# Attention in one run of 160 steps of 128 queries, with the row sums applied to the output through a product with the identity

## The chip, the core and the metric

The kernel runs on one core of a Trainium2 chip. The metric is the device time of one execution in microseconds; given is the median of the runs. TensorE's granted clock has two levels, 2.4 GHz (written 1.00) and 1.2 GHz (0.50).

## What is computed

The reference is a two-layer backbone over 1024 latent tokens and 256 context tokens, all in float32. The change lies in the even layer's mixer, which has two kinds of attention side by side, eight heads each: grouped queries with 64 dimensions a head and two shared key heads, and a low-rank form with 96 dimensions (64 + 32) and a key for each head. Latent queries see all 1280 tokens, context queries only the 256 context tokens. Cut to what matters:

```python
def attend(q, k, v, scale):
    s = jnp.einsum('bhgqd,bhkd->bhgqk', q, k).astype(jnp.float32) * scale
    p = jax.nn.softmax(s, axis=-1).astype(v.dtype)
    return jnp.einsum('bhgqk,bhkd->bhgqd', p, v)
```

Around it stand input and output projections, norms and an MLP, and a second layer of long convolutions and a state-space scan. They make up most of the time and are not touched.

## The kernel before

`attention` (L1039) works heads in pairs: four pairs of the first kind, then four of the second. The loop `for kind in range(2)` (L1083) opens a stage of its own for each kind, with its own tiles and semaphores and a barrier at its end. Each pair has 20 steps. A step is one head with 128 queries against all their keys; four steps (two heads, two halves of 256 queries) make a block. Steps 0 to 15 of a pair are wide (1280 keys), steps 16 to 19, the context queries, narrow (256 keys). Here "step" counts within the pair where a number below 20 is given.

What a step does, in the order of its data:

- Scores (L1151, TensorE): products with the query block as weights, in parts of 512, 512 and 256 keys, into three of PSUM's banks 0 to 5 (two sets by the step's parity). To keep float32 precision, queries and keys are split into a high and a low part; the first kind takes two products a part (its low query part shares the rows of the high one), the second kind three.
- Row maximum (L1209, VectorE), negated, out of the score banks.
- Exponential (L1265, ScalarE), into one of three buffers `probs`, with the row's sum beside it.
- Reciprocal of the sum (L1215) and scaling of the probabilities (L1217), both VectorE.
- Turning (L1165, TensorE): ten transposes of 128 x 128 in groups of four, four and two, each group into one of two banks, 6 and 7; ScalarE copies each group out (L1240). A group waits until the last but one user of its bank has been copied out.
- After the four steps of a block, the mix (L1177, TensorE): for each of 10 key tiles and both heads a product with 64 columns of `v` as weights and 256 columns of turned probabilities, the two heads in the two halves of the partitions of one bank; ScalarE copies the result into `mixed` (L1247).

Each engine's order is a loop over x, written out by hand. TensorE in turn x: the scores of step x (behind exponential x-2), the mix if one is due, the turning of step x-2. VectorE: maximum x, then reciprocal and scaling of x-1. ScalarE: the mix's copy, the three turning copies of x-2, exponential x, which also waits until the transposes of x-3 have read its buffer (L1261).

The next pair's queries and keys come in items: three of the first kind, four of the second. SyncE loads an item (L1123) and, once a pair, the values (L1130, L1132); ScalarE rounds it to the high part (L1230), VectorE subtracts to get the low part (L1199). Items stand in the loops at steps 5, 8, 11 (and 14) of a pair (`split_at`, L1107): ScalarE rounds behind exponential i, VectorE splits behind reciprocal and scaling of i-1. The last pair of each kind has none. The items of a kind's first pair come before its first step.

Each product in float32 (not those of rounded parts) leaves two records in the trace, a transpose one. Of products that the comparison in the prediction touches, L1619 and L1620 stand in the scan of the second layer, with 64 columns of weights and 128 moving columns, eight heads into alternating halves of the partitions, and L1569 copies a bank of 512 columns with VectorE.

Of the kernel before, what the change touches and what calls it, by code (L numbers as in the profile page):

```python
# [1038 lines left out]
def attention(nc, g, sc, out):  # L1039

    PAIRS = 4
    QB = 256

    steps = [(b, h, t) for b in range(TOK // QB) for h in range(2) for t in range(2)]  # L1050
    S, B = len(steps), TOK // QB
    PER_BLOCK = S // B
    ALL = [(pair, i) for pair in range(PAIRS) for i in range(S)]
    N = len(ALL)

    def keys_of(b):
        return (0, KTILES) if b < LAT // QB else (LAT // P, KTILES)

    def block_of(x):
        return steps[ALL[x][1]][0]  # L1060

    def width(x):
        lo, hi = keys_of(block_of(x))
        return (hi - lo) * P

    def turns(x):
        lo, hi = keys_of(block_of(x))
        return [(i, min(i + 4, hi)) for i in range(lo, hi, 4)]

    use = {}
    for x in range(2, N + 3):
        if x > 2 and (x - 2) % PER_BLOCK == 0:
            use["mix", (x - 3) // PER_BLOCK] = len(use)
        if x - 2 < N:
            for j in range(len(turns(x - 2))):
                use["turn", x - 2, j] = len(use)
# [4 lines left out]
    for kind in range(2):  # L1083
        rows = slice(0, (P, B_DK)[kind])

        items = (((0, 0), (0, 1), (1, 0)), ((0, 0), (0, 1), (1, 0), (1, 1)))[kind]
        I = len(items)
        COPIES = (2, 1)[kind]
        names = "raw_in0 raw_in1 v_in0 v_in1 rounded split scores maxed exped inverse probs filled emptied"
        with stage(nc, names) as (mem, sems):  # L1090
            raw_in, v_in, (rounded, split, scores, maxed, exped, inverse, probs, filled, emptied) = sems[:2], sems[2:4], sems[4:]
            raw = tile(nc, mem, "qk_raw", [P, 2, TOK])
            heads = len(items) - 2
            q_hi, k_hi, k_lo = (tile_r(nc, mem, f"{x}", [P, 2, n, TOK]) for x, n in (("q_high", 2), ("k_high", heads), ("k_low", heads)))
            q_lo = q_hi if kind == 0 else tile_r(nc, mem, "q_low_part", [P, 2, 2, TOK])
            v = tile(nc, mem, "v_pair", [P, 2, KTILES, 2, B_V])
            p = tile(nc, mem, "probs", [P, 3, TOK])
            pt = tile(nc, mem, "probs_turned", [P, 2, 2, KTILES, QB])
            neg_max, total, inv = (tile(nc, mem, f"row_{x}", [P, 4]) for x in ("max", "sum", "inv"))

            def source(pair, item):
                which, h = item
                if kind == 0:
                    return sc.qk_a[1 + pair][64 * h:64 * h + 64, :] if which == 0 else sc.qk_a[0][64 * (pair // 2):64 * (pair // 2) + 64, :]
                return (sc.q_b, sc.k_b)[which][2 * pair + h]

            def split_at(x):  # L1107

                pair, i = ALL[x]
                n, off = divmod(i - 5, 3)  # L1110
                return (pair + 1, n) if off == 0 and 0 <= n < I and pair + 1 < PAIRS else None

            with nc.Block() as block:
                @block.sync
                def _(sp):
                    for pair in range(PAIRS):
                        for n in range(I):
                            m = pair * I + n
                            if m >= 2:
                                sp.wait_ge(split, m - 1)  # L1120
                            for c in range(COPIES):
                                at = rows if kind == 1 else slice(64 * c, 64 * c + 64)
                                sp.dma_start(raw[at, m % 2, :], source(pair, items[n])).then_inc(raw_in[m % 2], 16)  # L1123
                        if pair >= 2:

                            sp.wait_ge(filled, use["mix", (pair - 1) * B - 1] + 1)
                        s = pair % 2
                        if kind == 0:
                            for h in range(2):
                                sp.dma_start(v[:, s, :, h, :], sc.v_a[:, :, 64 * (pair // 2):64 * (pair // 2) + 64]).then_inc(v_in[s], 16)  # L1130
                        else:
                            sp.dma_start(v[:, s], sc.v_b[:, :, 128 * pair:128 * pair + 128].rearrange("p j (h n) -> p j h n", h=2)).then_inc(v_in[s], 16)  # L1132

                @block.tensor
                def _(pe):
                    def scores_of(x):
                        pair, i = ALL[x]
                        b, h, t = steps[i]
                        s, q0 = pair % 2, b * QB + t * P
                        qs = slice(q0, q0 + P)  # L1140
                        lo, hi = keys_of(b)
                        parts = [(a, min(BANK, hi * P - a)) for a in range(lo * P, hi * P, BANK)]
                        if i == 0:
                            pe.wait_ge(split, I * (pair + 1))
                        if x >= 2:
                            pe.wait_ge(exped, x - 1)
                        kh = 0 if kind == 0 else h
                        passes = [(q_hi, k_hi), (q_hi, k_lo)] + ([(q_lo, k_hi)] if kind else [])
                        for j, (a, n) in enumerate(parts):
                            for m, (left, right) in enumerate(passes):  # L1150
                                mm = pe.matmul(g.ps[:, 3 * (x % 2) + j, 0:n], left[rows, s, h, qs], right[rows, s, kh, a:a + n],  # L1151
                                               start=(m == 0), stop=(m == len(passes) - 1))
                            if j == len(parts) - 1:
                                mm.then_inc(scores, 1)

                    def turn(x):
                        first = keys_of(block_of(x))[0]
                        for j, (lo, hi) in enumerate(turns(x)):
                            if j == 0:
                                pe.wait_ge(probs, x + 1)  # L1160
                            r = use["turn", x, j]
                            if r >= 2:
                                pe.wait_ge(emptied, r - 1)
                            for kt in range(lo, hi):
                                mm = pe.transpose(g.ps[:, 6 + r % 2, (kt - lo) * P:(kt - lo + 1) * P], p[:, x % 3, (kt - first) * P:(kt - first + 1) * P], g.ident[:])  # L1165
                            mm.then_inc(filled, 1)
# [1331 lines left out]
```

## Time and profile before

| | |
|---|---|
| median of 3 runs | 4337.72 us (4336.04 to 4343.98) |
| the profiled execution, own time | 4339.12 us |
| its span | 4337.3 us |
| TensorE products, busy | 3786.3 us (87%) |
| VectorE, busy | 1762.5 us (41%) |
| ScalarE, busy | 1252.4 us (29%) |
| mean granted TensorE clock | 0.933 |

The span runs from the first to the last instruction; the execution's own time is measured around it. Busy time is the union of an engine's instructions, and a product's record is longer than the time from its start to the next one's, since products are pipelined: for TensorE the distance of starts tells the pace.

### The profile page before, as it was taken

Reading aid. Unit: us, or ns where it says so; the run is one execution under the profiler, and the core shown is the slowest. Engines: PE = TensorE matmul, PEld = TensorE weight load, DVE = VectorE, ACT = ScalarE, POOL = GpSimd, SP = SyncE. Lnnn points to the kernel's source line nnn. Section 1 sums busy time; section 2 is a strip of 40 time slices with the busy share of each in tenths; the row PEclk is TensorE's granted clock in tenths of the full one; section 3 lists DMA queues with packets and bytes.
Section 4 is the critical chain, followed back from the end, with each engine's and each line's share of the span. In section 5 each row is a group of like instructions: output and inputs, shape, how many; then the busy total and the mean of one; then the engine's idle time right before and its main releaser. Section 6 shows DMA issues by size and latency. Waiting matters only on the chain. (4 is left out here: it accounts for less than half of the span.)

```text
span 4337.3 us, 44967 instructions
## 1 busy us (share of the span) xinstructions
PE 3786.3 (87%) x17768; PEld 2748.8 (63%) x17768; DVE 1762.5 (41%) x2399; ACT 1252.4 (29%) x2132; POOL 114.0 (3%) x80
## 2 busy tenths in 40 slices
PE   6987788789877999999987997759899778999997
PEld 3662466566656888888856685513344547888885
DVE  2223566455335333333354334952133234333334
ACT  3322577566433111111132132201100132221122
POOL 0000000000010000000010002200000010000001
PEclk8998899899988999999998998859999889999998
DMA  7623310200121111111122110021300121111112
GB/s 299 248 73 109 80 37 1 58 25 16 35 97 45 39 39 39 38 34 39 39 102 78 64 35 2 1 84 49 136 25 25 53 83 58 45 48 49 48 48 92
DMA packets 98139, 272.34 MB, mean 63 GB/s; under 512 B 18157, under 2 KB 33005, under 8 KB 93972
## 3 DMA queue, kind: packets, MB, share of 16 engines
q1 hardware_dynamic: 98004, 270.51, 18.8%
q8 instruction: 88, 1.44, 0.1%
q14 instruction: 47, 0.39, 0.0%
HBM read 220.41 MB, written 50.07 MB: 62 GB/s over the span
## 5 line engine op out<-in xcount | busy, mean ns | idle before, releaser
L569 PE MATMUL psum<-h_high,w_high 128*128 128x512 f32 (+1 forms) x1280 | 473.5, 370 | 51.7 <-DVE w_low L648 51.7
L569 PE MATMUL psum<-h_low,w_high 128*128 128x512 f32 (+1 forms) x1280 | 473.0, 370 | 0.0
L569 PE MATMUL psum<-h_high,w_low 128*128 128x512 f32 (+1 forms) x1280 | 472.5, 369 | 0.0
L582 PE MATMUL psum<-hid_low,w_high 128*128 128x512 f32 (+1 forms) x1280 | 471.5, 368 | 0.0
L582 PE MATMUL psum<-hid_high,w_high 128*128 128x512 f32 (+1 forms) x1280 | 471.3, 368 | 0.0
L582 PE MATMUL psum<-hid_high,w_low 128*128 128x512 f32 (+1 forms) x1280 | 470.8, 368 | 0.0
L513 PE MATMUL psum<-h_high,w_high 128*128 128x512 f32 (+1 forms) x944 | 367.8, 390 | 36.8 <-DVE w_low L506 24.6
L645 DVE TENSOR_TENSOR out<-out,psum 128x512 f32<-128x512 f32 x320 | 202.9, 634 | 463.2 <-PE psum L582 463.2
L513 PE MATMUL psum<-h_high,w_low 128*128 128x512 f32 (+1 forms) x944 | 349.4, 370 | 0.0
L513 PE MATMUL psum<-h_low,w_high 128*128 128x512 f32 (+1 forms) x944 | 349.1, 370 | 0.0
L595 ACT ACTIVATE w_high<-w_raw 128x1024 fp32r<-128x1024 f32 x126 | 132.7, 1053 | 663.2 <-PE psum L582 662.8
L569 PEld LDWEIGHTS psum<-h_high,w_high 128*128 128x128 f32 x1280 | 242.5, 189 | 93.7 <-DVE w_low L648 29.0
L635 DVE TENSOR_TENSOR hid_high<-hid_relu 128x512 fp32r<-128x512 f32 x160 | 102.3, 639 | 479.6 <-ACT hid_relu L610 479.6
L1209 DVE TENSOR_REDUCE row_max<-psum 128x1 f32<-128x1280 f32 (+1 forms) x160 | 204.2, 1276 | 184.8 <-PE psum L1151 180.6
L1165 PE MATMUL psum<-identity,probs 128*128 128x128 f32 x1344 | 214.3, 288 | 64.7 <-ACT probs_turned L1240 34.6
L569 PEld LDWEIGHTS psum<-h_low,w_high 128*128 128x128 f32 x1280 | 242.6, 190 | 40.3
L569 PEld LDWEIGHTS psum<-h_high,w_low 128*128 128x128 f32 x1280 | 242.4, 189 | 40.7
L582 PEld LDWEIGHTS psum<-hid_high,w_high 128*128 128x128 f32 x1280 | 241.4, 189 | 40.8
L582 PEld LDWEIGHTS psum<-hid_low,w_high 128*128 128x128 f32 x1280 | 241.4, 189 | 40.1
L582 PEld LDWEIGHTS psum<-hid_high,w_low 128*128 128x128 f32 x1280 | 241.1, 188 | 40.4
L610 ACT ACTIVATE hid_relu<-psum 128x512 f32<-128x512 f32 x160 | 89.0, 556 | 561.7 <-PE psum L569 561.7
L513 PEld LDWEIGHTS psum<-h_high,w_high 128*128 128x128 f32 x944 | 179.0, 190 | 76.7 <-DVE w_low L506 23.7
(312 smaller groups left out, 5539.2 us busy)
## 6 DMA issues: line engine op xcount, KB each, us to landing
w_raw<-in_ff_w_dram SPq DMA_DIRECT2D x128, 512.0 KB
ada_ring<-in_ada_w_dram SPq DMA_DIRECT2D x24, 2048.0 KB, 8.9
scratch_x<-x SPq DMA_DIRECT2D x6, 2048.0 KB, 7.2
x<-scratch_x SPq DMA_DIRECT2D x6, 2048.0 KB
x<-in_x_dram SPq DMA_DIRECT2D x4, 2048.0 KB, 11.4
w_raw<-in_w_out_dram SPq DMA_DIRECT2D x16, 512.0 KB
scratch_spectra<-spectrum_out SPq DMA_DIRECT2D x32, 256.0 KB, 2.0
filter_ring<-scratch_spectra SPq DMA_DIRECT2D x16, 512.0 KB, 3.7
```

The source lines that it names most:

```text
L513: mm = pe.matmul(out, x[:, k, :], y[:, k, a:a + n], start=(k == 0 and i == 0), stop=(k == KT - 1 and i == 2))
L569: mm = pe.matmul(g.ps[:, u % BANKS, 0:n], x[:, k, :], y[:, k, a:a + n], start=(k == 0 and i == 0), stop=(k == KT - 1 and i == 2))
L582: mm = pe.matmul(g.ps[:, BANKS + u % BANKS, 0:n], x[:, k * 2 + half, :], y[:, k, a:a + n], start=(k == 0 and i == 0), stop=(k == HT - 1 an ...
L595: act.activation(w_hi[:, slot], raw[:, slot], ACT.Copy).then_inc(w_rounded, 1)
L610: act.activation(relu[:, u % 2, 0:n], g.ps[:, u % BANKS, 0:n], ACT.Relu).then_inc(up_free, 1)
L635: dve.tensor_tensor(hid_hi[:, j, a:a + n], relu[:, u % 2, 0:n], relu[:, u % 2, 0:n], ALU.mult).then_inc(rounded, 1)
L645: dve.tensor_tensor(out[:, m, a:a + n], out[:, m, a:a + n], g.ps[:, BANKS + u % BANKS, 0:n], ALU.add).then_inc(down_free, 1)
L1165: mm = pe.transpose(g.ps[:, 6 + r % 2, (kt - lo) * P:(kt - lo + 1) * P], p[:, x % 3, (kt - first) * P:(kt - first + 1) * P], g.ident[:])
L1209: dve.tensor_reduce(neg_max[:, x % 4:x % 4 + 1], flat, AX.X, ALU.max, negate=True).then_inc(maxed, 1)
```

## The change

The two stages become one. Tiles are allocated once, with room for the larger kind, and all eight pairs run as one chain of 160 steps; a table gives each item a number over all pairs, so that the last pair of the first kind now carries the four items of the first pair of the second. A block is 128 queries of both heads, two steps; a mix comes every second step, with 128 moving columns.

The scaling of the probabilities goes. Instead, behind a block's mix, TensorE multiplies the identity by the reciprocals spread over 64 weight columns, which puts each query's reciprocal into its column, in columns 128 to 255 of the same bank. ScalarE copies the mix to `mix_raw`, VectorE multiplies it by that and writes `mixed`.

TensorE turns step x-3 in turn x of its loop and places the groups of transposes between the parts of the scores; ScalarE's exponential is that of step x-1 in turn x; VectorE copies out the first group of each step. The items stay at steps 5, 8, 11, 14: ScalarE rounds behind exponential i (in turn i+1), VectorE splits in turn i. Four semaphores take the place of `emptied`, so that a group of transposes or a mix waits for the engine that copied its bank.

```diff
-    PAIRS = 4
-    QB = 256
...
-    steps = [(b, h, t) for b in range(TOK // QB) for h in range(2) for t in range(2)]
+    PAIRS, KINDS = 4, 2
+    LAG = 3
+    HEADS = 2
+    B = TOK // P
+    S = B * HEADS
+    ALL = [(pair, i) for pair in range(KINDS * PAIRS) for i in range(S)]
...
-    for kind in range(2):
...
-        with stage(nc, names) as (mem, sems):
+    with stage(nc, names) as (mem, sems):
...
+                def bank_free(r):
+                    if r < 2:
+                        return
+                    key = user[r - 2]
+                    if key[0] == "mix":
+                        pe.wait_ge(mixed_out, key[1] + 1)
+                    elif key[2] == 0:
+                        pe.wait_ge(first_out, key[1] + 1)
+                    else:
+                        pe.wait_ge(turned_out, act_turns[key[1], key[2]] + 1)
...
+                def mix(y):
+                    pair, b, _ = step(2 * y)
+                    lo, hi = keys_of(b)
+                    r = use["mix", y]
+                    bank_free(r)
+                    pe.wait_ge(first_out, 2 * y + 2)
+                    if act_turns_until(2 * y + 1):
+                        pe.wait_ge(turned_out, act_turns_until(2 * y + 1))
+                    pe.wait_ge(v_in[pair % 2], v_total(pair))
+                    for kt in range(lo, hi):
+                        for h in range(HEADS):
+                            mm = pe.matmul(g.ps[64 * h:64 * h + 64, 6 + r % 2, 0:P], v[:, pair % 2, kt, h, :], pt[:, y % 2, h, kt, :],
+                                           start=(kt == lo), stop=(kt == hi - 1))
+                    pe.wait_ge(inverse, 2 * y + 2)
+                    for h in range(HEADS):
+                        at = (2 * y + h) % 8
+                        mm = pe.matmul(g.ps[64 * h:64 * h + 64, 6 + r % 2, P:2 * P], inv[:, at:at + 1].to_broadcast([P, 64]), g.ident[:], start=True, stop=True)
...
-                    for x in range(N + 3):
-                        if x < N:
-                            scores_of(x)
-                        if x > 2 and (x - 2) % PER_BLOCK == 0:
-                            mix((x - 3) // PER_BLOCK)
-                        if 2 <= x < N + 2:
-                            turn(x - 2)
+                for x in range(N + LAG + 3):
+                    late = 2 if x < N and kind_of(step(x)[0]) else 3
+                    if x < N:
+                        scores_of(x, 0, 1)
+                    turn_due(x, 0)
+                    if x < N:
+                        scores_of(x, 1, late)
+                    turn_due(x, 1)
+                    if x < N:
+                        scores_of(x, late, 3)
+                    if block_due(x) is not None:
+                        mix(block_due(x))
+                    turn_due(x, 2)
...
+                for x in range(N + LAG + 3):
+                    if 0 <= x - LAG < N:
+                        dst, src = turned_to(x - LAG, 0)
+                        dve.wait_ge(filled, use["turn", x - LAG, 0] + 1)
+                        dve.tensor_copy(dst, src).then_inc(first_out, 1)
+                    if x < N:
+                        dve.wait_ge(scores, x + 1)
+                        if x >= 4:
+                            dve.wait_ge(exped, x - 3)
+                        dve.tensor_reduce(neg_max[:, x % 4:x % 4 + 1], scores_flat(x), AX.X, ALU.max, negate=True).then_inc(maxed, 1)
+                    if block_due(x) is not None:
+                        y = block_due(x)
+                        pair, b, _ = step(2 * y)
+                        r = use["mix", y]
+                        dve.wait_ge(mix_copied, y + 1)
+                        dve.tensor_tensor(out[:, pair, b * P:(b + 1) * P], mix_raw[:, y % 2, :], g.ps[:, 6 + r % 2, P:2 * P], ALU.mult).then_inc(mixed_out, 1)
+                    if 1 <= x <= N:
+                        y = x - 1
+                        dve.wait_ge(exped, y + 1)
+                        if y >= 8:
+                            dve.wait_ge(filled, use["mix", (y - 8) // 2] + 1)
+                        dve.reciprocal(inv[:, y % 8:y % 8 + 1], total[:, y % 4:y % 4 + 1]).then_inc(inverse, 1)
+                    if x < N and split_at(x):
+                        split_item(*split_at(x))
...
-                            dve.tensor_scalar(p[:, y % 3, 0:width(y)], p[:, y % 3, 0:width(y)], inv[:, y % 4:y % 4 + 1], None, ALU.mult).then_inc(probs, 1)
...
+                for x in range(N + LAG + 3):
+                    if 1 <= x <= N:
+                        y = x - 1
+                        act.wait_ge(maxed, y + 1)
+                        if y >= 3:
+
+                            act.wait_ge(filled, last_turn(y - 3) + 1)
+                        if y >= 4:
+                            act.wait_ge(inverse, y - 3)
+                        act.activation(p[:, y % 3, 0:width(y)], scores_flat(y), ACT.Exp, bias=neg_max[:, y % 4:y % 4 + 1],
+                                       accum_out=total[:, y % 4:y % 4 + 1]).then_inc(exped, 1)
+                        if split_at(y):
+                            round_item(*split_at(y))
+                    for j in (1, 2):
+                        if j == 2 and block_due(x) is not None:
+                            y = block_due(x)
+                            r = use["mix", y]
+                            act.wait_ge(filled, r + 1)
+                            if y >= 2:
+                                act.wait_ge(mixed_out, y - 1)
+                            act.activation(mix_raw[:, y % 2, :], g.ps[:, 6 + r % 2, 0:P], ACT.Copy).then_inc(mix_copied, 1)
+                        if 0 <= x - LAG < N and j < len(turns(x - LAG)):
+                            dst, src = turned_to(x - LAG, j)
+                            act.wait_ge(filled, use["turn", x - LAG, j] + 1)
+                            act.activation(dst, src, ACT.Copy).then_inc(turned_out, 1)
```

## Rows read from the trace of the kernel before

**Rows 1.** Table of stretches: each engine's busy us (instructions), granted clock, DMA share, GB/s
```profile
456.00:1122.00 666.00, 554.61 (x3728) 416.21 (x3728) 381.95 (x508) 429.84 (x804) 0.00 (x0) 0.95 0.14 32
```

**Rows 2.** Timeline, wide steps of first kind: start, us, engine, line, count [idle before]
```profile
707.95 1.32 ACT L1265 ACTIVATE probs<-psum,row_max 128x1280 f32<-128x1280 f32 x1
...
711.45 4.54 PE L1177 MATMUL psum<-probs_turned,v_pair 128*64 128x256 f32 x40
715.92 1.78 PE L1165 MATMUL psum<-identity,probs 128*128 128x128 f32 x10
717.46 0.48 PE L1151 MATMUL psum<-k_high,q_high 128*128 128x512 f32 x1
...
718.71 1.03 PE L1165 MATMUL psum<-identity,probs 128*128 128x128 f32 x8
...
723.55 1.32 ACT L1265 ACTIVATE probs<-psum,row_max 128x1280 f32<-128x1280 f32 x1
```

**Rows 3.** Timeline, ScalarE, a block of the second kind
```profile
1055.66 1.32 ACT L1265 ACTIVATE probs<-psum,row_max 128x1280 f32<-128x1280 f32 x1
...
1073.50 1.32 ACT L1265 ACTIVATE probs<-psum,row_max 128x1280 f32<-128x1280 f32 x1
```

**Rows 4.** Timeline, the seam between the kinds
```profile
762.73 0.49 ACT L1265 ACTIVATE probs<-psum,row_max 128x256 f32<-128x256 f32 x1
...
785.04 0.79 PE L1151 MATMUL psum<-k_high,q_high 96*128 96x512 f32 x1 [19.09 <-DVE k_low L1199]
...
790.17 1.33 ACT L1265 ACTIVATE probs<-psum,row_max 128x1280 f32<-128x1280 f32 x1 [6.71 <-DVE row_max L1209]
```

**Rows 5.** Timeline, ScalarE: first and last exponentials of four pairs
```profile
623.02 1.33 ACT L1265 ACTIVATE probs<-psum,row_max 128x1280 f32<-128x1280 f32 x1 [0.92 <-DVE row_max L1209]
...
693.53 0.49 ACT L1265 ACTIVATE probs<-psum,row_max 128x256 f32<-128x256 f32 x1
...
696.48 1.33 ACT L1265 ACTIVATE probs<-psum,row_max 128x1280 f32<-128x1280 f32 x1 [0.93 <-DVE row_max L1209]
...
957.86 1.33 ACT L1265 ACTIVATE probs<-psum,row_max 128x1280 f32<-128x1280 f32 x1 [0.92 <-DVE row_max L1209]
...
1038.97 0.49 ACT L1265 ACTIVATE probs<-psum,row_max 128x256 f32<-128x256 f32 x1
...
1042.50 1.33 ACT L1265 ACTIVATE probs<-psum,row_max 128x1280 f32<-128x1280 f32 x1 [0.92 <-DVE row_max L1209]
...
1116.72 0.49 ACT L1265 ACTIVATE probs<-psum,row_max 128x256 f32<-128x256 f32 x1
```

**Rows 6.** Timeline, TensorE, scan of the second layer: first and last of eight rows
```profile
2706.28 0.45 PE L1619 MATMUL psum<-segments,x_dt 128*64 128x128 f32 x4 [0.36 <-DVE segments L1712]
...
2707.86 0.44 PE L1620 MATMUL psum<-exp_acs,states 128*64 128x128 f32 x4
```

**Rows 7.** Groups by line, VectorE, 2690 to 2760 us: busy us, mean ns, idle before
```profile
L1569 DVE COPY ssd_out<-psum 128x512 f32<-128x512 f32 x8 | 5.5, 684 | 0.0
```

**Rows 8.** Timeline, an item step of the first kind: rounding and split
```profile
504.45 1.27 ACT L1230 ACTIVATE q_high<-qk_raw 128x1280 fp32r<-128x1280 f32 x1
...
505.75 1.49 DVE L1199 TENSOR_TENSOR q_high<-qk_raw,q_high 64x1280 fp32r<-64x1280 f32 x1 [2.03 <-ACT q_high L1230]
```

**Rows 9.** Timeline, TensorE behind two of its longer stops, one in each kind
```profile
523.63 0.55 PE L1165 MATMUL psum<-identity,probs 128*128 128x128 f32 x3 [1.83 <-DVE probs L1217]
...
858.70 1.63 PE L1165 MATMUL psum<-identity,probs 128*128 128x128 f32 x8 [2.63 <-DVE probs L1217]
```

**Rows 10.** Table of stretches around such stops; the clock is the third number from the end
```profile
859.00:862.40 3.40, 3.40 (x19) 3.17 (x18) 1.88 (x5) 2.09 (x8) 0.00 (x0) 0.52 0.03 11
...
941.00:947.80 6.80, 5.25 (x24) 4.78 (x25) 3.69 (x9) 4.35 (x9) 0.00 (x0) 0.50 0.24 75
...
1026.30:1033.00 6.70, 6.00 (x28) 5.31 (x30) 2.87 (x7) 4.79 (x11) 0.00 (x0) 0.50 0.01 2
518.00:526.00 8.00, 4.60 (x30) 3.61 (x29) 6.21 (x7) 6.07 (x12) 0.00 (x0) 1.00 0.31 82
```

More of the change, by code:

```diff
@@ L1039, in attention @@
 def attention(nc, g, sc, out):
[L1047 to L1054 removed]
+    PAIRS, KINDS = 4, 2
[4 more added lines that the diff above has]
+    ALL = [(pair, i) for pair in range(KINDS * PAIRS) for i in range(S)]
+    N = len(ALL)
+    ITEMS = (((0, 0), (0, 1), (1, 0)), ((0, 0), (0, 1), (1, 0), (1, 1)))
@@ L1056, in keys_of, with kind_of, step @@
+    COPIES = (2, 1)
+    ROWS = (slice(0, P), slice(0, B_DK))
+    jobs = [(pair, n) for pair in range(KINDS * PAIRS) for n in range(len(ITEMS[pair // PAIRS]))]
+    job_of = {job: m for m, job in enumerate(jobs)}
+    def kind_of(pair):
+        return pair // PAIRS
+    def step(x):
+        pair, i = ALL[x]
+        return pair, i // HEADS, i % HEADS
     def keys_of(b):
-        return (0, KTILES) if b < LAT // QB else (LAT // P, KTILES)
-    def block_of(x):
-        return steps[ALL[x][1]][0]
+        return (0, KTILES) if b < LAT // P else (LAT // P, KTILES)
@@ L1062, in width, with raw_total @@
     def width(x):
-        lo, hi = keys_of(block_of(x))
+        lo, hi = keys_of(step(x)[1])
         return (hi - lo) * P
     def turns(x):
-        lo, hi = keys_of(block_of(x))
+        lo, hi = keys_of(step(x)[1])
         return [(i, min(i + 4, hi)) for i in range(lo, hi, 4)]
-    use = {}
-    for x in range(2, N + 3):
-        if x > 2 and (x - 2) % PER_BLOCK == 0:
[L1075 to L1078, printed above, removed]
+    def raw_total(m):
+        return 16 * sum(COPIES[kind_of(jobs[i][0])] for i in range(m % 2, m + 1, 2))
@@ new lines, in v_total, with block_due @@
+    def v_total(pair):
+        return 16 * sum(COPIES[kind_of(i)] for i in range(pair % 2, pair + 1, 2))
+    def block_due(x):
+        y, odd = divmod(x - LAG - 2, 2)
+        return y if not odd and 0 <= y < N // 2 else None
+    use, act_turns = {}, {}
+    for x in range(N + LAG + 3):
+        for j in range(3):
+            if j == 2 and block_due(x) is not None:
+                use["mix", block_due(x)] = len(use)
+            if 0 <= x - LAG < N and j < len(turns(x - LAG)):
+                use["turn", x - LAG, j] = len(use)
+                if j:
+                    act_turns[x - LAG, j] = len(act_turns)
@@ L1080, in last_turn @@
+    user = {r: key for key, r in use.items()}
     def last_turn(x):
         return use["turn", x, len(turns(x)) - 1]
-    for kind in range(2):
[L1084 to L1089, printed above, removed]
-        with stage(nc, names) as (mem, sems):
[L1091 to L1144, printed above, removed]
@@ L1145, in scores_of @@
                         if x >= 2:
                             pe.wait_ge(exped, x - 1)
[L1147 to L1166, printed above, removed]
@@ new lines, in scores_of @@
+                    kh = 0 if kind == 0 else h
+                    passes = [(q_hi, k_hi), (q_hi, k_lo)] + ([(q_lo, k_hi)] if kind else [])
+                    for j, (a, n) in list(enumerate(parts))[first:last]:
+                        for m, (left, right) in enumerate(passes):
+                            mm = pe.matmul(g.ps[:, 3 * (x % 2) + j, 0:n], left[at, s, h, qs], right[at, s, kh, a:a + n],
+                                           start=(m == 0), stop=(m == len(passes) - 1))
+                        if j == len(parts) - 1:
+                            mm.then_inc(scores, 1)
@@ new lines, in turn_due @@
+                def turn_due(x, j):
+                    if 0 <= x - LAG < N and j < len(turns(x - LAG)):
+                        turn(x - LAG, j)
+                for x in range(N + LAG + 3):
[11 more added lines that the diff above has]
+                    turn_due(x, 2)
```

188 lines of the change are left out of this document (107 added, 81 removed).

## The prediction

> **What bounds the kernel now.** The change touches attention alone. A table of stretches [rows 1] gives its part of the span, 456 to 1122 us: of 666 us matrix products are busy for 555, VectorE for 382, ScalarE for 430. No engine is full, so I looked for the wait that ends last in three places, each by the starts of the exponentials, one a step. **A steady block**: four steps of the first kind with one mix take 723.55 - 707.95 = 15.60 us [rows 2], of the second 1073.50 - 1055.66 = 17.84 [rows 3]. In the three steps without the mix the timeline shows TensorE stopping before its third group of transposes until a bank is copied out, and ScalarE with three copies and an exponential back to back; during the mix ScalarE has nothing to copy. TensorE sets one step and ScalarE's copies the other three. **The seam between the kinds**: the last exponential of the first kind starts at 762.73, the first of the second at 790.17, and TensorE is idle for 19.09 us of it [rows 4]. **The item steps**: three or four times in a pair a piece of the next pair's queries or keys is rounded by ScalarE and split by VectorE, and both queues stand behind it. From the first exponential of a pair to its last it is 70.51 us with three items and 66.25 without in the first kind, 81.11 with four and 74.22 without in the second [rows 4, 5].
>
> **The sum, part by part.** The profiled execution took 4339.1 us, 1.4 above the median of 4337.7. The sum is a difference, worked out within the profiled one and put on the median.
>
> *Mixing in blocks of 128 queries.* The 672 mix products become 1344 of half the width; each leaves two records. Today 40 records of 256 columns take 715.92 - 711.45 = 4.47 us, 0.112 each [rows 2]. The nearest row of the new shape, 64 weight columns against 128, is in the scan stage: two lines with 32 records of it together, from 2706.28 to 0.22 behind 2707.86, so 1.80 us, 0.056 each [rows 6]. 40 of them take 2.25 us, and column work stays the same: nothing gained or lost. The Trainium skill (TensorE: Matmul & The Clock Gate, Back-to-back issue gap) speaks against the change here: it says that a stream of weight loads and products of 128 columns keeps about 81 ns apiece. By that, as an estimate, the 2688 records would cost 67 us more; rows 6 disagree. *The product with the identity* adds four such records a block: 0.22 us in each of 80 blocks, all on TensorE. The reciprocals it reads were made long before, so I cost its wait at nothing.
>
> *Two steady steps.* First kind: scores 718.71 - 717.46 = 1.25 us, ten transposes 1.09 together (eight run for 1.03, the last one's own length among it, so I take 0.109 from start to start), so 4.68 for two steps; with 2.25 and 0.22 it is 7.15 us. With two turning banks some waits stay: a copy takes 0.6 to 0.7 us, and the group after next finds its bank full for 0.1 to 0.5. I laid the new queue orders out with these durations and find some 0.5 in two steps, 7.65 against 7.80 now. Second kind: nine products for six, scores 1.25 x 1.5 = 1.87, so 8.4 and 0.1 of waits, 8.5 against 8.92. There are 32 such pairs of steps of each kind: -5 and -13 us. Bounds: no wait left -38; 0.5 us more of waits in each two steps +14. I take -18, the layout being nearer the rows than either end, and +3.5 for the 16 narrow blocks, whose identity products buy nothing. VectorE loses a scaling of 1280 columns and gains a copy out of PSUM, 0.68 us [rows 7], and every second step a product of a quarter of its width, at most as much; ScalarE loses one copy of three. The maximum has the width of a split, 1.49 [rows 8], so VectorE has under 2.7 us of work in 3.8: cost nothing. TensorE covers it; with that cover gone VectorE would set 2.7 a step.
>
> *One run of 160 steps.* The 27.44 us at the seam become what lies between two pairs, 696.48 - 693.53 = 2.95 [rows 4, 5]: -24.5. Bounds: -24.5 and 0, if pair 3 cannot take its neighbour's pieces in time. I take -24.5, since other pairs do it. SyncE issues the same transfers in the same order, and none is moved past another.
>
> *Items.* Now 9 at (70.51 - 66.25) / 3 = 1.42 us and 12 at 6.89 / 4 = 1.72: 33 us. Afterwards there are 25, as pair 3 also carries the four of pair 4. This is where the new order hurts. VectorE meets the split of step i right behind that step's maximum and stands until ScalarE has rounded. ScalarE rounds behind exponential i, and that, through its wait for the buffer of three steps ago, cannot start before TensorE's last transposes of the same turn of the loop, nor, by its queue, before their copy. From there on: copy of 256 columns 0.3 (a fifth of the 1.32 of 1280), exponential 1.32, rounding until VectorE starts 505.75 - 504.45 = 1.30, split 1.49, and then the next step's first copy, 0.68, which was ScalarE's and now stands behind the split: 5.0 us with the ends overlapping by 0.1 [rows 2, 7, 8]. On TensorE the mix or the third transposes wait for that bank, and all else is queued behind. Before them TensorE has a step's scores and two groups, 2.1 us (2.5 to 2.7 in the second kind). So it stands 2.9 or 2.5 us, and 3.5 where the next step has a mix (items at steps 8 and 14), since ScalarE's own copies are then 0.6 behind. The first kind has 8 and 5 of these, the second 6 and 6: 8 x 2.9 + 5 x 3.5 + 6 x 2.5 + 6 x 3.5 = 77 us, net +44. Bounds: as dear as today, 25 x 1.5 = 38, net +5; nothing beside the chain, 25 x 5.0, net +92. I take the chain less the work beside it.
>
> Together: -18 + 3.5 - 24.5 + 44 = +5 us.
>
> *The clock.* In the narrow steps of the second kind TensorE stood for 2.63 us before 858.70, and the granted clock was half (0.5, 1.2 GHz) from 859.1 for 3.4 us; at the same place of the next two pairs it was half for 6.8 and 6.7. After a stop of 1.83 us before 523.63 it stayed 1.00 [rows 9, 10]. Of the new stops 13 of the first kind and 6 of the second are longer than 2.63, six a little shorter. I take 17 falls. In 3.4 to 6.8 us at half clock TensorE loses 1.7 to 3.4 where it is the limit; some of it runs in the next wait, so 2.1 each: +36 us. Bounds: no fall, 0; 25 falls at 2.8, +70.
>
> Forecast: +41 on 4337.7, **4379 us**.
>
> **Rivals.** (1) *The clock holds*: the new stops lie in dense work, the narrow steps in thin. For it: 1.83 us did nothing. Against it: all three such places in the second kind were answered. Then +5, 4343 us; chance 0.20. (2) *Faster: the item steps hide their chain.* Its place is VectorE's first copy, its price what that copy is late for its bank. At today's 1.5 us an item with the clock unmoved the sum is -18 + 3.5 - 24.5 + 5 = -34, 4304 us; it decides as soon as an item costs under 2.8 us. For it: today's items hide half of their work. Against it: today only the next maximum stands behind the split, then a bank does. Chance 0.10. (3) *Narrow products don't stream.* If a record keeps the 0.112 us of today's, the 2688 add 0.056 x 2688 = 150; half of that gives 4454 us. Against it: rows 6, with the same alternation of halves. Chance 0.05. The skill's 81 ns would be in this case. (4) *The seam stays*, since pair 4's pieces come late: 24 us more, 4403 us. Against it: their steps are 5, 8, 11 and 14 of 20. Chance 0.05.
>
> **Numbers.** The forecast keeps 0.60. A measurement of this kernel tells a change of 0.2% (8.7 us, 4329 to 4346) from none. Case 1 lies in that band for 0.14 of its 0.20, with 0.02 faster and 0.04 slower. Faster: 0.10 + 0.02 = 0.12; same 0.14; slower 0.60 + 0.04 + 0.10 = 0.74. The range goes down to 4338, which takes in most of case 1 and leaves out case 2, and up to 4402, the forecast with 59 of the clock's 70 us, which leaves out cases 3 and 4.
>
> **What would show it.** Mix records of 128 columns 0.056 us apart; TensorE idle for 2.5 to 3.5 us once behind each item and for over 1 us hardly elsewhere; VectorE's split waiting longer for the rounding than now; half clock behind most items; first-kind pairs some 80 us long, the last pair without items under 76. It is wrong if pairs with three items last under 75 us, if the clock stays full behind the items, or if mix records lie over 0.07 us apart.

## The result, and the profile after

| | before | after |
|---|---|---|
| median | 4336.88 us, 4 runs | 4383.66 us (4379.17 to 4388.61), 4 runs |
| ratio | 1 | 1.0103 [1.0087, 1.0119] |
| profiled execution, span | 4337.3 us | 4379.5 us (own time 4381.26) |
| attention, first score to last `mixed` | 648.2 us | 691.1 us |
| the rest of the kernel behind it | 3216.1 us | 3215.5 us |
| first exponential of a pair to the next pair's, first kind | 73 | 82 us |
| half clock behind a stop in attention | 3, in the narrow steps of the second kind | 23, behind 25 item stops |

The kernel became slower by 1.03%; 4379 had been forecast. All of it is in attention, +42.9 us. (The untouched rest lay between 3208 and 3220 us over the profiles of this study, so the experiments are read by attention's own length wherever the total is too coarse.)

Two words are used throughout. A *stop* is a stretch in which TensorE stands still and waits. A *fall* is a stretch at half clock that follows: the granted clock goes from 1.00 to 0.50 and comes back after 3.4 us, sometimes 6.8.

The page after, engines:

```profile
span 4379.5 us, 48447 instructions
PE 3825.9 (87%) x19432; PEld 2836.1 (65%) x19432; DVE 1752.0 (40%) x2479; ACT 1184.2 (27%) x2012; POOL 114.0 (3%) x80
```

Attention as a stretch, to be held against [rows 1]; then the stretch behind one item's stop, and behind the two stops, of 3.33 and 2.43 us, that no fall followed. Columns: length, busy us of TensorE, its weight loads, VectorE, ScalarE and GpSimd, granted clock, DMA share, GB/s.

```profile
456.00:1164.00 708.00, 593.81 (x5392) 503.10 (x5392) 371.44 (x588) 361.61 (x684) 0.00 (x0) 0.92 0.13 31
594.00:597.80 3.80, 3.39 (x36) 3.39 (x38) 1.75 (x2) 0.00 (x0) 0.00 (x0) 0.55 0.67 172
790.20:793.60 3.40, 3.23 (x48) 2.87 (x49) 1.71 (x3) 0.64 (x3) 0.00 (x0) 1.00 0.53 149
830.40:834.00 3.60, 3.59 (x29) 3.10 (x31) 2.60 (x4) 2.35 (x4) 0.00 (x0) 1.00 0.44 137
```

VectorE has 10 us less work than before and ScalarE 68 less, and the stretch is 42 longer. TensorE's busy time grew with it (554.6 to 593.8 us) and is 83 to 84% of it in both. No engine is fuller: something waits more. TensorE's waits say for what (in total, times, longest):

```profile
PE psum L1192 <- DVE probs_turned L1262: 43.5, 30, 3.0
PE psum L1206 <- DVE probs_turned L1262: 40.6, 19, 3.5
...
PE psum L1192 <- ACT probs_turned L1321: 0.8, 3, 0.3
```

84 us of idle TensorE end with the same instruction, VectorE's copy of a step's first group of transposes; 76 of them are the 25 stops behind items. ScalarE's copies, which set three of four steps before, end next to none. The timeline of one item (rows left out are marked; all engines, start and length; the idle time before and who ended it in brackets):

```profile
573.62 0.44 PE L1192 MATMUL psum<-identity,probs 128*128 128x128 f32 x2
574.09 0.38 ACT L1321 ACTIVATE probs_turned<-psum 128x256 f32<-128x256 f32 x1
574.37 1.33 ACT L1306 ACTIVATE probs<-psum,row_max 128x1280 f32<-128x1280 f32 x1
...
575.64 0.60 PE L1192 MATMUL psum<-identity,probs 128*128 128x128 f32 x4
575.68 1.27 ACT L1293 ACTIVATE q_high<-qk_raw 128x1280 fp32r<-128x1280 f32 x1
576.98 1.49 DVE L1254 TENSOR_TENSOR q_high<-qk_raw,q_high 64x1280 fp32r<-64x1280 f32 x1 [2.57 <-ACT q_high L1293]
578.50 0.69 DVE L1262 COPY probs_turned<-psum 128x512 f32<-128x512 f32 x1
579.25 0.44 PE L1192 MATMUL psum<-identity,probs 128*128 128x128 f32 x2 [3.00 <-DVE probs_turned L1262]
```

Read it downwards as one chain: TensorE's last transposes of a turn, their copy, the exponential, the rounding, the split, the copy that had to wait behind the split, and TensorE again. VectorE stood for 2.57 us with the bank's copy in its queue (its group of transposes had left TensorE at 575.64 + 0.60) and nothing to do but wait for ScalarE. From the start of the last transposes to the third transposes of the next turn it is 5.6 us, of which TensorE stands for 3.00.

A steady two steps of the first kind, by ScalarE's exponentials, and the seam between the kinds (before: [rows 2] and [rows 4]):

```profile
517.16 1.32 ACT L1306 ACTIVATE probs<-psum,row_max 128x1280 f32<-128x1280 f32 x1
520.15 1.33 ACT L1306 ACTIVATE probs<-psum,row_max 128x1280 f32<-128x1280 f32 x1 [0.21 <-DVE row_max L1267]
524.81 1.33 ACT L1306 ACTIVATE probs<-psum,row_max 128x1280 f32<-128x1280 f32 x1
...
805.74 0.47 ACT L1306 ACTIVATE probs<-psum,row_max 128x256 f32<-128x256 f32 x1
...
809.28 1.33 ACT L1306 ACTIVATE probs<-psum,row_max 128x1280 f32<-128x1280 f32 x1 [2.97 <-DVE row_max L1267]
```

Steady: 524.81 - 517.16 = 7.65 us. Seam: 3.54 us where 27.44 were.

### The profile page after: what moved, and what is told of

The parts are those of the page before. It is cut to its first block and busy times, and to the rows that moved or that the text cites. A ratio compares the mean times of both kernels' runs of the same rounds, so it can differ in the third digit from the quotient of the medians.

```text
span 4379.5 us, 48447 instructions
## 1 busy us (share of the span) xinstructions
PE 3825.9 (87%) x19432; PEld 2836.1 (65%) x19432; DVE 1752.0 (40%) x2479; ACT 1184.2 (27%) x2012; POOL 114.0 (3%) x80
## 5 line engine op out<-in xcount | busy, mean ns | idle before, releaser
L1192 PE MATMUL psum<-identity,probs 128*128 128x128 f32 x1344 | 224.8, 287 | 48.5 <-DVE probs_turned L1262 43.5
L1192 PEld LDWEIGHTS psum<-identity,probs 128*128 128x128 f32 x1344 | 161.6, 145 | 106.2 <-DVE probs_turned L1262 50.4
```

## The experiments

The theory at this point: attention is made of four effects (steady steps a little faster, seam gone, item chains through VectorE's queue, half clock behind the chains' stops). The rival for the two dear ones: the narrow products and the extra waits on two banks cost it, and the clock only goes with it. Each ratio is to the kernel before, with its 95% interval; kernels that ran together share a chip and its runs of before.

### The split one turn later

The edit leaves every instruction as it is. VectorE meets the split of step i behind the first copy and the maximum of step i+1, when the rounding has long been done.

```diff
-                    if x < N and split_at(x):
-                        split_item(*split_at(x))
+                    if 1 <= x <= N and split_at(x - 1):
+                        split_item(*split_at(x - 1))
```

> The changed kernel with one edit: VectorE splits an item one turn of its loop later, behind the first copy and the maximum of the next step; ScalarE's rounding stays where it is. Theory A (an item holds VectorE's first copy, that holds a turning bank and TensorE, and each such stop of 2.4 to 3.5 us is followed by half clock): the 25 stops go, the falls with them, 25 x 3.07 and some 36 to 42 us of clock less about 0.2 an item for the work itself: about 4284 us, some 53 below the kernel before, TensorE nowhere idle for over 1 us between the first and last pair, ratio to before 0.988. Theory B (the loss sits in the narrower blocks, the identity products and the two banks): within 10 us of 4384.

Measured: 4275.49 us (4273.64 to 4280.59), ratio 0.9852 [0.9836, 0.9868]; attention 590.3 us, 101 less than after. The same place as above, in that trace:

```profile
563.35 1.27 ACT L1293 ACTIVATE q_high<-qk_raw 128x1280 fp32r<-128x1280 f32 x1
563.51 1.49 DVE L1267 TENSOR_REDUCE row_max<-psum 128x1 f32<-128x1280 f32 x1
...
565.10 1.49 DVE L1254 TENSOR_TENSOR q_high<-qk_raw,q_high 64x1280 fp32r<-64x1280 f32 x1
565.25 0.63 PE L1192 MATMUL psum<-identity,probs 128*128 128x128 f32 x4 [0.66 <-ACT probs_turned L1321]
...
567.37 0.33 PE L1206 MATMUL psum<-probs_turned,v_pair 128*64 128x128 f32 x2 [0.35 <-DVE probs_turned L1262]
```

The split no longer waits (it starts 0.48 us behind the rounding's end, because VectorE was busy), TensorE's stops are 0.66 and 0.35 us, and in the steps the clock is never half. The time is 9 us under the expected 4284. Two instructions' order in one queue was worth 2.5% of the kernel (1.0103 - 0.9852; by attention's length 101 us, 2.3%), over twice what the change lost. The rival is out: the narrow products and the banks are the same here.

### Useless work in the stop

Here the stops' length is taken away and their time left. In the step behind an item TensorE computes 19 score products into columns 256 to 511 of the third score bank, of which the true scores fill only the first 256 and which nobody reads. They take 2.3 us, so that TensorE works while the chain runs.

```diff
+                        if j == 2 and x >= 1 and split_at(x - 1):
+                            for _ in range(19):
+                                pe.matmul(g.ps[:, 3 * (x % 2) + 2, 256:512], q_hi[at, s, h, qs], k_hi[at, s, kh, 0:256], start=True, stop=True)
```

> The changed kernel with 19 products of 256 columns, whose result nobody reads, put before the last part of the scores in the step behind each item: 2.2 us more work for TensorE, in the time in which it stands. Theory A: the chain through VectorE is as long as before, so the steps behind items keep 5 us, but TensorE's idle time falls under 1.3 us and the clock stays: the 24 falls of the changed kernel cost nothing any more, 4384 - 40 = 4344 us, ratio to before about 1.002. Rival (half clock falls into waits and costs nothing): 4384 us or more. Rival (TensorE is the limit there): 4384 + 25 x 2.2 = 4439 us.

Measured: 4338.83 us (4331.6 to 4342.8), ratio 0.9994 [0.9984, 1.0004]; attention 652.6 us. TensorE in the place of one stop, and attention as a stretch:

```profile
581.85 2.44 PE L1169 MATMUL psum<-k_high,q_high 128*128 128x256 f32 x19
...
584.36 0.60 PE L1195 MATMUL psum<-identity,probs 128*128 128x128 f32 x4
586.15 2.40 PE L1209 MATMUL psum<-probs_turned,v_pair 128*64 128x128 f32 x40 [1.19 <-DVE probs_turned L1265]
588.38 0.39 PE L1214 MATMUL psum<-identity,row_inv 128*64 128x128 f32 x4
```
```profile
456.00:1124.00 668.00, 611.86 (x5867) 526.07 (x5867) 370.76 (x588) 361.58 (x684) 0.00 (x0) 0.98 0.14 33
```

475 useless products made attention 38.5 us shorter, 0.9% of the kernel (1.1% by the totals, in which the rest of the kernel came out 6 us shorter too). The chains are as long as after, but of the 25 stops the 11 in front of a mix are 1.06 to 1.21 us and the others under 0.8, and no half clock follows one. That is the clock's price by itself: 38.5 / 23 falls = 1.7 us each. Pair by pair against this kernel a fall of 3.4 us cost 1.4 to 1.6 us and one of 6.8 cost 2.7. What stays, 652.6 against the 648.2 of before, is all the rest of the change: +4.4 us. The mix records stand here at full clock: 40 in 588.38 - 586.15 = 2.23 us, 0.056 each.

### Fewer useless products

The same with 8 in place of 19: stops between those of the two kernels.

> e2 with 8 products in place of 19: 0.93 us of work in the step behind each item, so that TensorE stands about 2.55 us where the changed kernel stands 3.47, 2.0 for 2.9 and 1.5 for 2.4. If a stop's length decides on the fall alone (2.63 fell, 1.83 did not): the 11 longest go one way together, 11 falls or none, and their places repeat. If the alignment of a stop counts too: some of them, 4 to 9 falls, differing from pair to pair. At 1.6 us a fall: 4384 - 1.6 x 17 = about 4356 us, 4345 to 4366.

Measured: 4351.87 us (4347.53 to 4355.52), ratio 1.0022 [1.0013, 1.0032]; attention 670.1 us. The time was forecast well (4356); the falls were one more than the 4 to 9 expected: 11 stops are 2.4 to 2.5 us long, 8 about 2.0 and 6 about 1.5, and 4, 5 and 1 of them were followed by half clock, 10 of 25. Two of them, each with the stretch behind it:

```profile
609.27 0.44 PE L1195 MATMUL psum<-identity,probs 128*128 128x128 f32 x2 [1.94 <-DVE probs_turned L1265]
...
997.50 0.44 PE L1195 MATMUL psum<-identity,probs 128*128 128x128 f32 x2 [1.48 <-DVE probs_turned L1265]
```
```profile
609.30:613.00 3.70, 3.70 (x40) 3.31 (x42) 3.53 (x4) 2.29 (x4) 0.00 (x0) 1.00 0.72 180
998.00:1001.40 3.40, 3.40 (x13) 2.68 (x12) 1.61 (x3) 1.78 (x3) 0.00 (x0) 0.51 0.44 130
```

The longer stop was let go, the shorter one was not, and the same place of another pair does otherwise. A stop's length doesn't decide it alone: at nearly the same length the stops of 2.43 us of the changed kernel were followed by a fall in 5 of 6 cases, those of 2.39 to 2.52 us here in 4 of 11. Over the kernels together length does change how often: none of 25 up to 1.21 us, 10 of 25 from 1.5 to 2.5, 23 of 25 from 2.4 to 3.5. The price per fall agrees. There is an eleventh in the first steps, at 479 us, before any item, so (670.1 - 652.6) / 11 = 1.6 us.

### The first copy by ScalarE

The change had moved one copy of three from ScalarE to VectorE. Here ScalarE makes it (same copy, same semaphore; in its queue behind the exponential and the rounding, ahead of its own two copies), so that no bank hangs on the split.

```diff
-                    if 0 <= x - LAG < N:
-                        dst, src = turned_to(x - LAG, 0)
-                        dve.wait_ge(filled, use["turn", x - LAG, 0] + 1)
-                        dve.tensor_copy(dst, src).then_inc(first_out, 1)
...
+                    if 0 <= x - LAG < N:
+                        dst, src = turned_to(x - LAG, 0)
+                        act.wait_ge(filled, use["turn", x - LAG, 0] + 1)
+                        act.activation(dst, src, ACT.Copy).then_inc(first_out, 1)
```

> The changed kernel with one edit: the first group of transposes is copied out by ScalarE again, as the two others; VectorE keeps everything else and its split stays. Theory A: no bank hangs on VectorE, the stops at items fall under 2 us and the clock stays, but ScalarE with exponential, three copies and every second step the mix has over 3.1 us a step: about 4354 us, 17 above before. Theory B (not VectorE's copy): stops and falls stay and ScalarE's load comes on top, 4384 us or more.

Measured: 4355.83 us (4349.16 to 4361.11), ratio 1.0031 [1.0021, 1.0041]; attention 665.3 us. The item steps shrink (stops up to 2.02 us, four falls in all, one of them in the first steps, before any item), but each steady two steps of the first kind now take 5.27 + 3.00 = 8.27 us in place of 7.65. So the copy on VectorE was worth having; only what stood ahead of it in the queue was wrong.

### The kernel before in one run

The other half of the question, what the seam alone gives. Tiles and item numbers as in the change; blocks of 256 queries, scaling, copies and queue orders of before.

```diff
-    ALL = [(pair, i) for pair in range(PAIRS) for i in range(S)]
+    KINDS = 2
+    ALL = [(pair, i) for pair in range(KINDS * PAIRS) for i in range(S)]
...
-    for kind in range(2):
...
-                return (pair + 1, n) if off == 0 and 0 <= n < I and pair + 1 < PAIRS else None
+                return (pair + 1, n) if off == 0 and pair + 1 < KINDS * PAIRS and 0 <= n < len(ITEMS[kind_of(pair + 1)]) else None
```

> The kernel before with one part of the change alone: both kinds in one stage and one run of 160 steps, blocks of 256 queries, scaling and all orders as before. If the seam is worth what I took: 27.4 us between the exponentials become 3, less four items more at about 1.5: 4337 - 24.5 + 6 = 4318 us. If the seam stays because the pieces come late: 4337 to 4343 us.

Measured: 4328.28 us (4324.42 to 4334.51), ratio 0.9973 [0.9963, 0.9983]; attention 638.9 us, 9.3 less than before. A miss by 10 us, and the most useful one. The seam gave its 24 us (3.53 from exponential to exponential). Pair 3 with its four items took 80.3 us to the next pair's first exponential, where its steps and such a passage took 66.25 + 2.95 = 69.2 before [rows 4, 5]: 11.1 given back. And the three pairs ahead of it took 74.3 to 75.0 us in place of 72.4 to 73.5, without a changed instruction: 5.0 us in all, which with the 5 that pair 3 took above the expected 6 make up the miss. In all four pairs the clock falls. One of the places:

```profile
600.19 1.09 PE L1179 MATMUL psum<-identity,probs 128*128 128x128 f32 x8 [1.82 <-DVE probs L1233]
```
```profile
601.90:605.30 3.40, 3.40 (x13) 2.24 (x13) 1.83 (x2) 1.77 (x4) 0.00 (x0) 0.50 0.00 0
```

It is the stop of 1.83 us of [rows 9], behind which the prediction had found the clock at 1.00 [rows 10]. In this kernel it falls in all four pairs (at 526.8, 601.9, 677.0 and 752.1), and the step then takes 8.9 us in place of 7.34: 1.55 us each. In pair 3 it falls once more, at 765.7 for 6.8 us, at its fourth item.

### Before, profiled again

Nothing is changed; one look.

> The kernel before unchanged, for a second profile. In its first one the nine stops of 1.83 us in the first kind left the clock alone; in e4 the same stops lowered it in four pairs. If alignment decides: here or there one of the nine (or the stops of 2.63 us spared), and the time within 4330 to 4350. If length decides: none of the nine, all three of 2.63 us.

Measured: 4338.16 us, attention 647.9. The stop of 1.83 us, one in each of the three pairs with items (three, and not nine as the expectation says): half clock behind one of them, none behind the other two.

```profile
594.88 2.16 PE L1165 MATMUL psum<-identity,probs 128*128 128x128 f32 x10 [1.83 <-DVE probs L1217]
```
```profile
595.40:598.80 3.40, 3.40 (x14) 2.78 (x12) 1.78 (x3) 2.81 (x5) 0.00 (x0) 0.52 0.34 78
521.00:526.00 5.00, 4.33 (x32) 3.29 (x34) 4.28 (x7) 3.60 (x7) 0.00 (x0) 1.00 0.37 89
669.00:674.00 5.00, 4.21 (x32) 3.16 (x34) 4.32 (x6) 3.73 (x7) 0.00 (x0) 1.00 0.02 3
```

So the same instruction of the same kernel is spared in one execution and caught in another. What tells them apart beyond the stop itself, no run shows.

### The later split in the two kernels of the old order

To split the rest of the gain, the edit of the first experiment was made in the kernel before and in its one-run form.

```diff
-                        if x < N and split_at(x):
-                            split_item(*split_at(x))
+                        if x >= 1 and split_at(x - 1):
+                            split_item(*split_at(x - 1))
```

> The kernel before with e1's edit alone: VectorE splits an item one turn later. If the block on VectorE is what its items cost there too (1.4 to 1.7 us at 21 items, half clock among it): some 15 to 25 us below before, 4320 us, with no idle time of 2.6 us left in the second kind and no half clock there. If those 33 us were the work of the rounding on ScalarE, the limit of that kernel: 4337.

Measured: 4317.03 us (4314.11 to 4321.73), ratio 0.9944 [0.9928, 0.9961]; attention 627.3 us, -20.9, which is 1.0 us for each of the 21 items, the clock included: the three falls in the narrow steps are gone. The kernel before had the same fault, in a milder form.

> e4 (the kernel before in one run) with e1's edit: blocks of 256 queries, scaling of the probabilities, no interleaving. e4 is at 0.9973 of before; its 25 items and eight stretches of half clock should give back 30 to 40 us: about 4295. What then lies between this and e1 (4275), some 20 us, is the worth of the narrower blocks, the interleaved transposes and the scaling moved to the output. If it reaches 4275 the new order is worth nothing once the items are mended.

Measured: 4300.66 us (4296.59 to 4302.22), ratio 0.9901 [0.9885, 0.9918]; attention 607.7 us. From here to the first experiment's 590.3 only the blocks of 128, the scaling moved to the output through the product with the identity, and the new queue orders differ: they are worth 17.4 us together.

### Without the product with the identity

The later split, and the mix is written out unscaled: the products with the identity are left out, and VectorE takes the maximum of the copied mix and the mix, an instruction of the same size. The rows are not divided by their sums.

```diff
-                    pe.wait_ge(inverse, 2 * y + 2)
-                    for h in range(HEADS):
-                        at = (2 * y + h) % 8
-                        mm = pe.matmul(g.ps[64 * h:64 * h + 64, 6 + r % 2, P:2 * P], inv[:, at:at + 1].to_broadcast([P, 64]), g.ident[:], start=True, stop=True)
...
-                        dve.tensor_tensor(out[:, pair, b * P:(b + 1) * P], mix_raw[:, y % 2, :], g.ps[:, 6 + r % 2, P:2 * P], ALU.mult).then_inc(mixed_out, 1)
+                        dve.tensor_tensor(out[:, pair, b * P:(b + 1) * P], mix_raw[:, y % 2, :], g.ps[:, 6 + r % 2, 0:P], ALU.max).then_inc(mixed_out, 1)
```

> As e1, without the product with the identity: VectorE writes the larger of the mix's copy and the mix itself, the same shapes and sources, so the output is left unscaled. If TensorE is the limit in steady steps, 80 blocks give back 0.18 to 0.22 us each: 14 to 18 us below e1 (4275), about 4260. If the product runs in a wait for a bank: 4275.

Measured: 4265.37 us (4262.85 to 4270.32), ratio 0.9824 [0.9808, 0.984]; attention 576.1 us against 590.3, so 14.2 / 80 = 0.18 us a block, close to the 0.22 of its four records.

### The items on GpSimd

GpSimd is idle in attention. First it takes the splits of all pairs but the first, in a queue of its own (waits as in VectorE's); then the rounding too. The first edit, shortened:

```diff
-                    if x < N and split_at(x):
-                        split_item(*split_at(x))
+            @block.gpsimd
+            def _(pool):
...
+                    pool.wait_ge(rounded, m + 1)
+                    pool.wait_ge(split, m)
...
+                    pool.tensor_tensor(low[at, s, h, :], raw[at, m % 2, :], high[at, s, h, :], ALU.subtract).then_inc(split, 1)
```

> The changed kernel with the splits of all items but the first pair's on GpSimd, in a queue of their own; rounding stays on ScalarE. Theory A: VectorE is never held, so no stop and no fall, and its 1.49 us an item go as well: 10 to 15 us below e1, about 4262, GpSimd taking some 2.6 us an item by its 1.05 for 512 columns in the scan. Rival (GpSimd beside VectorE slows VectorE): copies and maxima over 5% longer than in the changed kernel and no gain over e1, 4275 or more.

Measured: 4268.93 us (4262.85 to 4272.88), ratio 0.9828 [0.9811, 0.9844]; attention 581.9 us, 8.4 less than with the later split, where 10 to 15 had been expected.

> As e8, with the rounding on GpSimd too, so that neither ScalarE nor VectorE sees an item behind the first pair's: the steps behind items, 0.35 us longer in the first kind and 0.15 in the second in e8, become as the others: 13 x 0.35 + 12 x 0.15 = 6 us below e8 (4269), about 4262. If GpSimd is too slow at it (2.9 us for a split, rounding perhaps 1.5 to 3): 25 items take 150 us of a run of 580, no loss.

Measured: 4266.65 us (4264.81 to 4268.93), ratio 0.9827 [0.981, 0.9843]; attention 576.7 us, 5.2 less than with the splits alone, where 6 had been expected; the totals don't tell the two apart. All wide steps are steady ones now (4.66 and 3.00, 4.52 and 3.88). Groups of GpSimd in this kernel, then of VectorE in the one with the splits alone on GpSimd (count, busy us, mean ns, idle before):

```profile
L1291 POOL CAST q_high<-qk_raw 96x1280 fp32r<-96x1280 f32 x8 | 10.0, 1249 | 219.8 <-PE psum L1168 219.3
L1305 POOL TENSOR_TENSOR k_low<-qk_raw,k_high 96x1280 fp32r<-96x1280 f32 x8 | 23.5, 2931 | 0.6
```
```profile
L1262 DVE COPY probs_turned<-psum 128x512 f32<-128x512 f32 x128 | 88.0, 688 | 68.6 <-PE psum L1192 68.6
```

A split takes GpSimd 2.92 us, twice VectorE's 1.49, and it costs nothing: it has a pair's whole length for it, and no bank of PSUM stands behind it. VectorE's copies kept their 688 ns. By attention's length this is the fastest form with the full computation, 13.6 us below the later split; by the totals the intervals of these two (0.9843 at most, 0.9836 at least) still overlap. It stands 2.7% under the kernel after (0.9827 / 1.0103) and 1.7% under the one before.

## Why the prediction was right

It was 4379, measured 4383.66, inside the range of 4338 to 4402. Its steps, one by one:

- **Narrow mix products**, "0.056 each": 0.056 measured, so no cost. The Trainium skill's 81 ns apiece (TensorE: Matmul & The Clock Gate, Back-to-back issue gap) did not show in this stream of 64-column weights. Rival 3 is out.
- **The product with the identity**, 0.22 us a block: 0.18.
- **Steady steps**, "7.65 against 7.80" and "8.5 against 8.92": 7.65 and 8.40. With the narrow blocks -14.5 was forecast. Measured where no item disturbs the steps: a pair of the first kind takes 65.4 us from its first to its last exponential (items on GpSimd) where pair 3 took 66.25 before, one of the second kind 70.73 (the last pair) where it took 74.22. Four of each make -17.4, and the comparison with the later split on both sides gives -17.4 too.
- **Seam**, -24.5: 27.44 to 3.54 us, -23.9. Rival 4 is out.
- **Items**, "2.9, 3.5, 2.5 us" of stop and 77 in all: the stops are 2.87 to 3.01, 3.33 to 3.47 and 2.43. For the sum, the kernel with filled stops has the chains and no falls, the one with the items on GpSimd has no chains and a single fall, at 480 us, in its first steps: 652.6 - 576.7 = 75.9 us, and some 1.5 more for that fall, since its first pair took 69.2 us and the next 68.3 where with filled stops it is 77.0 and 77.6. So about 77. The first experiment shows that the place named, the first copy behind the split, is the cause. Rival 2 named the same place and said it would be hidden; it wasn't, at 3.0 to 3.1 us an item where it needed less than 2.8.
- **The sum without the clock**, +5 us: +4.4 in attention, by the filled stops.
- **The clock**, +36 as 17 falls at 2.1: mis-sized in both factors. There were 23 falls, at 1.7 us, 38.5 in all, so the product was near by two errors that cancel; that is luck. Why more falls: of the 19 stops longer than 2.63 us 18 were followed by one, and of the six "a little shorter", at 2.43, five. The count of 17 stood on three stops of 2.63 and one place with 1.83, read as a bound between them. The runs show no such bound: a stop of 1.83 us was followed by half clock four times in four in the one-run form and once in six in the two traces of the kernel before; one of 1.48 was, one of 3.33 (at 790.20) was not. Why cheaper: 20 of the falls lasted 3.4 us and three 6.8, and 2.1 lies between what the two cost, 1.4 to 1.6 and 2.7. TensorE would lose 1.7 and 3.4 if it were the limit throughout; that the difference ran in waits that the steps have anyway is likely and not shown. Rival 1 (the clock holds) is what the kernel with filled stops is: 4338.83 us where 4343 was put on it.

Put together: seam -23.9, items 77 - 33 = +44, clock +38.5, steady and narrow steps -17.4: +41 of the +42.9 measured. The 33 us for the items of before are read from [rows 4, 5] and have its three falls in them. Some 2 us stay open.

What the prediction asked to be seen was there: pairs with three items 82 us (80 forecast), the last pair without items 71 us to its last exponential (under 76), half clock behind 23 of 25 items. It had not asked the question that the first experiment answered, how much of the 113 us of chains and falls was there only for the place of one instruction. The time to ask was when the chain was written out: its dearest link, VectorE standing 2.57 us for ScalarE, was an order and no dependence.

## What to carry to other kernels

When work moves to another engine, look at what stands ahead of it in that queue: an instruction that waits for a third engine hands its wait to everything behind it, and here a bank of PSUM, and with it TensorE, hung on what stood behind. Put such side work where its input has long been made, even a whole step later, or on an engine nobody waits for, even one at half the speed. A stop of TensorE cost here more than its length: of 2.4 to 3.5 us, 1.7 us of clock on top in 23 cases of 25; of 1.5 to 2.5 us, in 10 of 25. One spared stop is no bound.

## What the runs showed of the hardware

- Work with no use sped the kernel up: 25 times 2.3 us of products in TensorE's stops took 38.5 us off attention, since the clock stayed at 1.00.
- A fall of the clock is not a property of the stop: in two executions of the kernel before, the 1.83 us stop of the second pair was spared once and caught once. A stop of 1.48 us was followed by 3.4 us at 0.51, one of 3.33 us by 1.00. And a fall needs no stop as long as these: in the kernel with the items on GpSimd the clock went to 0.50 at 480 us for 3.4 us, behind stops of 0.93 and 0.69 us in attention's first steps, where with filled stops those of 0.90 and 0.72 us were let go.
- GpSimd's subtraction of 1280 columns took 2.92 us beside VectorE's work out of PSUM, and VectorE's did not get longer: 688 ns a copy with the splits on GpSimd, 687 without. The Trainium skill (SBUF — State Buffer, Who interferes with whom) says that a VectorE instruction with at most one SBUF input, outside its two-port modes, does not contend with GpSimd; VectorE's copies, maxima and output products in these steps read PSUM and at most one input from SBUF, and with that the trace agrees.
